# Moving the token sums of a paired projection by five slots in a layer's mixing stage

## The reference

```python
h = rmsnorm(x, mix_norm[l])
proj = h @ w_in[l]                                   # 2048 rows; 1 column group = 512 columns
cq, ckv, kpe, hq, hf, hi, hg = jnp.split(proj, IN_SPLITS, axis=-1)
a = mla_group(cq, ckv, kpe, ...)                     # attention
r = hgrn2_group(hq, hf, hi, hg, ...)                 # gated recurrence, from hf the decays
x = x + jnp.concatenate([a, r], axis=-1) @ w_out[l]
```

## Time and profile before

| | us |
|---|---|
| three executions, median (lowest to highest) | 1884.99 (1883.53 to 1885.43) |
| the profiled execution, its own time | 1883.42 |
| its span, first to last instruction | 1881.6 |
| TensorE (PE) busy | 1874.3 |
| VectorE (DVE) busy | 1599.2 |
| ScalarE (ACT) busy | 1094.7 |
| GpSimd (POOL) busy | 93.5 |

### The profile page before, as it was taken

How to read it: one execution, slowest core, us unless ns; L and a number is a source line. 1 busy time by engine, 2 the same in 40 slices (tenths; PEclk the granted TensorE clock), 3 DMA queues, 4 the chain that set the end, 5 groups by cost and what they waited for, 6 DMA issues and landing times.

```text
span 1881.6 us, 23322 instructions
## 1 busy us (share of the span) xinstructions
PE 1874.3 (100%) x8811; PEld 1571.3 (84%) x8811; DVE 1599.2 (85%) x2060; ACT 1094.7 (58%) x1487; POOL 93.5 (5%) x98
## 2 busy tenths in 40 slices
PE   9999999999999999999999999999999999999999
PEld 7888888888889888888888888888888888888987
DVE  6999999989999867786676764789999999999986
ACT  7665555555656547556476655656555555555553
POOL 0000000000000001302250000000000000000000
PEclk9999999999999999999999999999999999999999
DMA  9666555656556665455443654455655566655654
GB/s 338 224 197 200 195 197 195 224 202 201 180 186 213 217 227 155 148 190 191 136 156 112 212 190 135 156 187 195 200 188 194 201 207 216 202 198 183 196 193 172
DMA packets 176689, 362.58 MB, mean 193 GB/s; under 512 B 8512, under 2 KB 19776, under 8 KB 175936
## 3 DMA queue, kind: packets, MB, share of 16 engines
q1 hardware_dynamic: 176144, 360.89, 57.5%
q10 hardware_dynamic: 432, 0.19, 0.0%
HBM read 358.95 MB, written 2.10 MB: 192 GB/s over the span
## 4 chain that ended last, share of the span: by engine, by line
PE 94%; DVE 4%; issue 1%; ACT 0%; DMA 0%; POOL 0%; DVEq 0%; SPq 0%; ACTq 0%
PE acc L2087 18%; PE acc L2089 18%; PE acc L2088 18%; PE acc L2076 8%; PE acc L2078 8%; PE acc L2077 8%; PE small L2087 2%; PE small L2089 2%; PE small L2088 2%; DVE w_lo L1374 2%; PE tr L2035 2%; PE small L2288 1%; PE tr L2089 1%; PE tr L2087 1%; PE tr L2088 1%; PE tr L2103 1%
## 5 line engine op out<-in xcount | busy, mean ns | idle before, releaser
L1374 DVE TENSOR_TENSOR w_lo<-w_raw,w_hi 128x1024 fp32r<-128x1024 f32 (+3 forms) x776 | 757.7, 1030 | 55.5 <-ACT w_hi L764 43.3
L764 ACT ACTIVATE w_hi<-w_raw 128x1024 fp32r<-128x1024 f32 (+4 forms) x562 | 499.5, 924 | 135.9 <-PE acc L2089 104.6
L2087 PE MATMUL acc<-w_hi,hT_hi 128*128 128x512 f32 (+1 forms) x966 | 373.2, 386 | 0.0
L2089 PE MATMUL acc<-w_lo,hT_hi 128*128 128x512 f32 (+1 forms) x966 | 371.3, 384 | 0.0
L2088 PE MATMUL acc<-w_hi,hT_lo 128*128 128x512 f32 (+1 forms) x966 | 371.0, 384 | 0.0
L869 ACT ACTIVATE w_hi<-w_raw 128x1024 fp32r<-128x1024 f32 (+1 forms) x190 | 196.7, 1045 | 123.8 <-DVE w_raw L1362 74.6
L1303 DVE TENSOR_TENSOR w_lo<-w_raw,w_hi 128x1024 fp32r<-128x1024 f32 (+1 forms) x166 | 198.9, 1239 | 31.8 <-ACT w_hi L764 30.4
L2087 PEld LDWEIGHTS acc<-w_hi,hT_hi 128*128 128x128 f32 x966 | 181.4, 188 | 34.4 <-DVE w_lo L1374 0.5
L2089 PEld LDWEIGHTS acc<-w_lo,hT_hi 128*128 128x128 f32 x966 | 181.3, 188 | 34.4
L2088 PEld LDWEIGHTS acc<-w_hi,hT_lo 128*128 128x128 f32 x966 | 181.5, 188 | 33.6
L862 ACT ACTIVATE w_hi<-w_raw 128x512 fp32r<-128x512 f32 (+3 forms) x190 | 154.1, 831 | 91.9 <-PE acc L2089 89.6
(11 more groups left out here) (344 smaller groups left out, 2611.4 us busy)
## 6 DMA issues: line engine op xcount, KB each, us to landing
w_raw<-in_ffn_w_down SPq DMA_DIRECT2D x56, 768.0 KB, 4.6
w_raw<-in_ffn_w_down SPq DMA_DIRECT2D x40, 1024.0 KB, 5.2
w_raw<-in_w_in SPq DMA_DIRECT2D x30, 1024.0 KB, 5.1
w_raw<-in_ffn_w_gate SPq DMA_DIRECT2D x58, 512.0 KB, 3.9
w_raw<-in_ffn_w_gate SPq DMA_DIRECT2D x38, 768.0 KB, 4.3
w_raw<-in_ffn_w_up SPq DMA_DIRECT2D x38, 768.0 KB, 4.6
w_raw<-in_ffn_w_up SPq DMA_DIRECT2D x54, 512.0 KB, 4.7
w_raw<-in_ffn_w_up SPq DMA_DIRECT2D x26, 1024.0 KB, 6.0
```

The costliest lines, as they stand in the source:

```text
L764: nc.scalar.activation(piece(w_hi, c % SPLIT, k0, k1, width), piece(raw, c % RAW, k0, k1, width), ACT.Copy).then_inc(hi_done, 1)
L1374: v.tensor_tensor(piece(w_lo, c % RAW, k0, k1, width), piece(raw, c % RAW, k0, k1, width), piece(w_hi, c % SPLIT, k0, k1, width).bitcast(F ...
L2087: mm(dst, lhs_hi, wh, start=first, stop=False)
L2089: return mm(dst, lhs_hi, wl, start=False, stop=last)
```

## The change

The sums of unit n are made by VectorE in slot 15 + n and not in slot 10 + n, rounded by ScalarE in slot 16 + n and not 11 + n, and split by VectorE in slot 17 + n and not 12 + n. Nothing else is edited.

```diff
@@ scalar, mixer(m)
-                if m in (11, 12, 13):
-                    act.wait_ge(ev("mix_sums_made"), m - 10)
-                    nc.scalar.activation(mS_hi[:, m - 11], mS_sum[:, m - 11], ACT.Copy).then_inc(ev("mix_sums_hi"), 1)
+                if m in (16, 17, 18):
+                    act.wait_ge(ev("mix_sums_made"), m - 15)
+                    nc.scalar.activation(mS_hi[:, m - 16], mS_sum[:, m - 16], ACT.Copy).then_inc(ev("mix_sums_hi"), 1)
@@ vector, mixer(m)
-                if m in (10, 11, 12):
-                    n = m - 10
+                if m in (15, 16, 17):
+                    n = m - 15
                     if n:
                         dve.wait_ge(ev("mix_sums_made"), n)
                     done(v.tensor_tensor(mS_flat[:], hT_hi[:, 2 * n:2 * n + 2, :].bitcast(F32), hT_lo[:, 2 * n:2 * n + 2, :].bitcast(F32), ALU.add))
                     done.wait()
                     token_sums(mS_sum[:, n, 0, :], [mS_sum[:, n, i, :] for i in range(1, 4)], mS_flat, "mix_sums_made")
-                if m in (12, 13, 14):
-                    n = m - 12
+                if m in (17, 18, 19):
+                    n = m - 17
                     dve.wait_ge(ev("mix_sums_hi"), n + 1)
                     v.tensor_tensor(mS_lo[:, n], mS_sum[:, n], mS_hi[:, n].bitcast(F32), ALU.subtract).then_inc(ev("mix_sums_split"), 1)
```

## The result

The changed kernel takes 1887.31 us (median of 21 executions, 1887.04 to 1888.51), the kernel before, timed again beside it, 1883.80 (median of 21, 1883.20 to 1886.12). The profiled execution took 1887.29 us, its span is 1885.5 (before: 1881.6, so 3.9 more).

What follows compares the result with a forecast made beforehand. TensorE, busy 1874.3 of 1881.6 us, bounds the kernel, so only its waits count. Delays carried through slots 15 to 18, 1.7, 3.09, 3.65 and about 3.7 us late, were taken as +3.5: 1888.5 us, range 1886.3 to 1890.4.

Steps and rivals of the forecast that it cites:

- waits for VectorE's copies: TensorE's waits for PSUM copies in the mixing stage: four of about 1.7, 2.6, 0.6, 0 to 0.1 us, replacing one.
- steps 3 to 5: Decay steps TensorE runs in the mixing stage; forecast to start 1.7, 3.09 and 3.65 us late.
- The relief in slot 14: Removing a split there spares GpSimd a delay, so VectorE's products start 0.48 us earlier, at 773.02.
- Slot 15: VectorE's weight split 1.5 us, sums with two GpSimd meetings 3.6; copy at 779.3, step 3 waits 1.7 us.
- Slot 16: VectorE 1.3 us late plus sums of 1.79: its copy and step 4 3.09 us late, step 4 at 788.2.
- Slot 17: Sums, one split and one GpSimd meeting add 3.29 us against a margin of 2.73: step 5 3.65 us late.
- Slot 18 and on: Added 3.7 us against margin 3.64 at step 6, nothing or 0.1; slot 19 covered, VectorE catching up in the following pair.
- The small instructions: The sums' 128-column instructions in VectorE: if GpSimd delays them too, total 3.5 us; if only wide ones, about 0.4.
- The first: Rival: the sums' small instructions are not held up, so the total is +0.4 to +1.5 us, about 1886; chance 0.15.
- The second: Rival: slots 18 and 19 do not catch up, giving +4.4 to +5.3 us, about 1890; chance 0.16.
- The third: Rival: clock falls to 1.2 GHz between steps 4 and 5, up to +7.8 us more, 1896; chance 0.03.
- Two signs: Forecast wrong if the granted clock falls, or TensorE's sum of waits grows by under 2 us or over 5.

Runs made afterwards that it cites:

- h_16_17: Changed kernel with the first unit's sums left in slot 10 (rounded in 11, split in 17), the others in slots 16 and 17; 1886.73 us, ratio 1.0019.
- c_slot17: Changed kernel with only one unit's sums late (made in slot 17, rounded in 18, split in 19); 1883.89 us, ratio 1.0003 against the kernel before.
- j_lo13: Kernel before with only the third unit's split moved from slot 14 to slot 13; 1882.34 us, ratio 0.9992.
- d_between: Changed kernel with VectorE's PSUM copy put between the halves of the weight split in slots 15 to 19; 1883.71 us, ratio 0.9999 against the kernel before.
- k_fills_after: Changed kernel with GpSimd's subtractions of steps 3 to 8 replaced by four constant fills that read nothing; 1882.94 us.
- the kernels with fills: Kernel before and changed kernel, GpSimd's subtractions of steps 3 to 8 replaced by constant fills: two fills 1881.93 and 1882.04 us, four fills 1881.86 and 1882.94.
- b_slot16: Changed kernel with only one unit's sums late (made in slot 16, rounded in 17, split in 18); 1886.65 us, ratio 1.0014 against the kernel before.
- e_before_between: Kernel before with VectorE's PSUM copy put between the two halves of the weight split in slots 15 to 19; 1882.34 us, ratio 0.9992.

## Why the prediction was right

The forecast was +3.5 us by the waits for VectorE's copies, 1888.5 us; measured are +3.5 and 1887.31. The path was right: the sums ahead of the copies of slots 15 to 17, and GpSimd's instructions that they meet, set the starts of steps 3 to 5. That it agrees to the tenth is partly luck. The slots' terms came to 3.65, rounded down to 3.5, and the starts show 3.72; the medians give 3.5 since the kernel before's own includes executions with a fall of the clock (against those at full clock it is 3.8). The difference in the total is in the base: of the three executions shown, with 1884.99 as their median, two lay at 1885.0 and 1885.4, where in the later runs only executions with a fall of the clock lie; over 21 the median is 1883.80.

**The relief in slot 14** was put at 0.48 and was 0.26 (products at 773.26, not 773.50, with step 2 at +0.02). GpSimd's half at 769.86 still takes 1.28 us, not 1.11. In slot 15 VectorE's second half of the split, which I had ahead of GpSimd, still met it (2.52 us and not 1.5), and the sums met it once and not twice: the two errors cancel, the copy stands at 779.54 where 779.3 was forecast.

**Slot 15.** Step 3 late by 1.7: measured 1.95, the 0.25 more being the relief that was smaller.

**Slot 16.** Step 4 late by 3.1: measured 3.14. The wait of 2.6 us that I forecast ahead of it is 0.76, though: 1.6 us went into slot 15's matmuls at half clock, and 0.2 was gone with step 3's longer wait.

**Slot 17.** 0.56 over the margin, step 5 late by 3.65: measured 3.65. The term over the margin is 0.51 here (3.65 less 3.14) and 0.5 in `h_16_17`, by the copy. It is no fixed price of the slot: in `c_slot17`, where nothing ahead of it is late, the same sums cost 1.3 us against `j_lo13`. The one GpSimd instruction more per slot is in the rows (1.52 us at 792.72, where 0.69 is free).

**Slot 18 and on.** 3.7 against 3.64: step 6 is 3.72 late, 0.07 after step 5. Slot 19 and the pair cover the rest, as forecast.

**The small instructions.** I took the rule of the Trainium skill ("SBUF — State Buffer", "SBUF: two separate sides") for them against no row: in `d_between` they are held up by 0.9 and 0.7 us like the wide ones. The same section limits this to GpSimd instructions that read; the fills in `k_fills_after` hold nothing up, so this half agrees as well. In the changed kernel itself the forecast of 1.2 us for one of them in slot 15 didn't come true: in slots 15 to 17 the wide first instruction (1.53, 1.53, 1.52) met GpSimd each time, and the small ones never did. So the assumption that I made to choose between 0.4 and 3.5 us was never put to use there; the 0.9 was right, the instruction that pays it was another.

**The rivals.** The first (cover holds, +0.4 to +1.5) is about what the kernels with fills do, +0.1 and +1.1, in which nothing is held up. But it hung on the small instructions alone, and these did not decide. The second (slots 18, 19) didn't occur. The third, the clock, did, though a step earlier and behind a shorter wait than I had placed it; I gave it a chance of 0.03, and the mean clock of all 21 executions shows it. I had it cost up to 7.8 us where a fall costs 1.6, and in the traced execution nothing. That it fell where a later wait covered it is luck: in `h_16_17` 1.15 us of it came out. I also read from the one traced execution of before that a wait of 1.19 leaves the clock full; 9 of 33 later executions have a mean of 0.999. Two signs that I named as refuting the forecast came true: the granted clock fell, and the sum of TensorE's waits grew by 1.6 us, under my 2, while the time grew as forecast. The sum of waits was the wrong quantity; the steps' starts were the right one.

What I did not see: that slot 16's wait in the kernel before hung on which of two instructions began first, 0.03 us apart. It was in the rows, and `j_lo13`, which moves one instruction of 0.68 us by one slot, is 1.3 us faster.

## What to carry to other kernels

Work that is moved along an in-order queue costs what it puts ahead of the next instruction that the bounding engine waits for, less the margin there, so read that margin slot by slot; with that instruction put ahead of the work the same work cost 3.6 us less here. Where VectorE and GpSimd both read SBUF, count instructions that meet, here at 0.7 to 0.95 us each, and look who starts first: VectorE 0.03 us behind GpSimd met two, 0.22 us ahead of it one. Compare the starts of a bounding engine's steps and not its list of waits, since a wait can turn into slower work.

## What the runs showed that I had not expected

A wait of TensorE of 1.15 to 2.7 us may be followed by a fall of the granted clock from 2.4 to 1.2 GHz that costs about 1.6 us. Three traces show one, behind waits of 1.76, 1.15 and 2.68 us. By the mean clock and the time, the kernel before, with a wait of 1.19, has it in 9 of 33 executions, `b_slot16`, with 2.7, in 8 of 11; with all waits for the copies gone, `j_lo13` and `e_before_between` have it in none of 22, and spread over 0.4 and 0.7 us where the kernel before spreads over 2.7. Nor is it in the 51 executions of `d_between` and of the kernels with fills, whose waits in this stage are 0.66 us at most. The Trainium skill ("TensorE: Matmul & The Clock Gate", "Part 1") has the clock fall after idleness, and the three traces agree that far. So a wait costs more than its length in some executions, and removing a wait of 1.2 us also removed most of the scatter. What decides in which executions it falls, no run here shows; nor is the wait alone proved to be the cause, since a wait of 1.0 us that all these kernels have in another stage brings no fall.
